# Softmax weights left unscaled in the three attention stages and turned by products with a scaled identity instead of transposes

## The reference

```python
def sink_softmax(logits, sink):
    m = jnp.maximum(jnp.max(logits, -1, keepdims=True), sink)
    e = jnp.exp(logits - m)
    return e / (jnp.sum(e, -1, keepdims=True) + jnp.exp(sink - m))
...
    orr = (jnp.einsum('bnkgim,bmkd->bnikgd', p[..., :N_META], vm)
           + jnp.einsum('bnkgij,bnjkd->bnikgd', p[..., N_META:], vband))
...
        p = jax.nn.softmax(jnp.concatenate([l_sel, l_own], axis=-1), axis=-1)
        o = (jnp.einsum('hqnj,hqnjd->hqd', p_sel, v_g.astype(jnp.float32))
             + jnp.einsum('hqk,hkd->hqd', p_own, v_own.astype(jnp.float32)))
```

## Time and profile before

| | us |
|---|---|
| median of 3 runs | 1254.89 |
| lowest, highest run | 1254.25, 1257.13 |
| the profiled execution | 1257.42 |
| its span, first to last instruction | 1255.6 |
| PE busy in the span | 1227.6 |
| DVE busy | 872.0 |
| ACT busy | 671.9 |

### The profile page before, as it was taken

How to read it: one execution, slowest core, us unless ns; L and a number is a source line. 1 busy time by engine, 2 the same in 40 slices (tenths; PEclk the granted TensorE clock), 3 DMA queues, 4 the chain that set the end, 5 groups by cost and what they waited for, 6 DMA issues and landing times.

```text
span 1255.6 us, 27652 instructions
## 1 busy us (share of the span) xinstructions
PE 1227.6 (98%) x10492; PEld 1194.4 (95%) x10492; DVE 872.0 (69%) x1585; ACT 671.9 (54%) x1210; POOL 179.5 (14%) x214
## 2 busy tenths in 40 slices
PE   7999999999999989999999999999999999999997
PEld 7889999999999879999999999999999879999997
DVE  7687578777645869888656667866455797766443
ACT  7766445555433756555545555655444586655432
POOL 0343050000012224000011004100011105000100
PEclk9999999999999999999999999999999999999999
DMA  7323257765544236555644444655555523655552
GB/s 290 102 86 102 85 159 211 209 194 197 195 149 145 85 106 215 185 183 192 225 170 132 138 152 136 202 184 185 184 187 182 185 85 117 201 184 180 189 186 68
DMA packets 60455, 205.89 MB, mean 164 GB/s; under 512 B 6096, under 2 KB 14544, under 8 KB 60240
## 3 DMA queue, kind: packets, MB, share of 16 engines
q1 hardware_dynamic: 56048, 200.33, 49.1%
q10 hardware_dynamic: 4320, 4.35, 1.1%
HBM read 200.46 MB, written 4.19 MB: 163 GB/s over the span
## 4 chain that ended last, share of the span: by engine, by line
PE 87%; DVE 7%; ACT 3%; issue 1%; DMA 1%; POOL 0%; ACTq 0%; DVEq 0%; SPq 0%
PE bank L317 27%; PE bank L319 26%; PE bank L318 26%; DVE w_lo L271 1%; DVE cb L684 1%; PE bank L1623 1%; PE bank L1613 1%; PE bank L1600 1%; DMA raw<-w_mix_in 1%; ACT w_hi L262 1%; ACT sm_s L1680 1%; DVE sm_d L1638 0%; PE bank L1269 0%; ACT sm_d L1680 0%; PE bank L1275 0%
## 5 line engine op out<-in xcount | busy, mean ns | idle before, releaser
L271 DVE TENSOR_TENSOR w_lo<-raw,w_hi 128x1024 fp32r<-128x1024 f32 (+1 forms) x357 | 458.1, 1284 | 195.1 <-ACT w_hi L262 194.5
L262 ACT ACTIVATE w_hi<-raw 128x1024 fp32r<-128x1024 f32 (+1 forms) x357 | 386.4, 1085 | 286.7 <-PE bank L319 278.5
L317 PE MATMUL bank<-x_hi,w_hi 128*128 128x256 f32 (+2 forms) x1776 | 511.4, 288 | 8.1 <-DVE x_lo L393 7.8
L319 PE MATMUL bank<-x_hi,w_lo 128*128 128x256 f32 (+2 forms) x1776 | 505.2, 284 | 0.0
L318 PE MATMUL bank<-x_lo,w_hi 128*128 128x256 f32 (+2 forms) x1776 | 505.1, 284 | 0.0
L317 PEld LDWEIGHTS bank<-x_hi,w_hi 128*128 128x128 f32 x1776 | 336.2, 189 | 10.5 <-DVE w_lo L271 7.7
L319 PEld LDWEIGHTS bank<-x_hi,w_lo 128*128 128x128 f32 x1776 | 336.1, 189 | 0.0
L318 PEld LDWEIGHTS bank<-x_lo,w_hi 128*128 128x128 f32 x1776 | 335.2, 189 | 0.5
L317 PE MATMUL bank<-m_hi,w_hi 128*128 128x256 f32 x512 | 144.1, 281 | 0.0
L318 PE MATMUL bank<-m_lo,w_hi 128*128 128x256 f32 x512 | 144.1, 281 | 0.0
L319 PE MATMUL bank<-m_hi,w_lo 128*128 128x256 f32 x512 | 144.1, 281 | 0.0
(11 more groups left out here) (331 smaller groups left out, 1686.9 us busy)
## 6 DMA issues: line engine op xcount, KB each, us to landing
raw<-w_up SPq DMA_DIRECT2D x88, 512.0 KB, 3.4
raw<-w_mlp_up SPq DMA_DIRECT2D x64, 512.0 KB, 4.2
raw<-w_mlp_down SPq DMA_DIRECT2D x64, 512.0 KB, 3.4
raw<-w_down SPq DMA_DIRECT2D x32, 704.0 KB, 4.0
raw<-w_mix_in SPq DMA_DIRECT2D x29, 512.0 KB, 3.4
raw<-w_moba_in SPq DMA_DIRECT2D x24, 512.0 KB, 3.7
raw<-w_swa_in SPq DMA_DIRECT2D x12, 512.0 KB, 3.3
raw<-w_mix_out SPq DMA_DIRECT2D x8, 512.0 KB, 3.2
```

The costliest lines, as they stand in the source:

```text
L262: nc.scalar.activation(w_hi[:, slot, 0:WIDTHS[g]], raw[:, slot, 0:WIDTHS[g]], ACT.Copy).then_inc(hi_ready, 1)
L271: nc.vector.tensor_tensor(w_lo[:, slot, 0:WIDTHS[g]], raw[:, slot, 0:WIDTHS[g]], w_hi[:, slot, 0:WIDTHS[g]].bitcast(F32), ALU.subtract).th ...
L317: nc.tensor.matmul(out, whi, xh, start=(chunk == 0), stop=False)
L319: mm = nc.tensor.matmul(out, wlo, xh, start=False, stop=end)
```

## The change

The exponentials stay as ACT wrote them. DVE builds, for each head and query group, a diagonal matrix: the identity times the reciprocal of each row's sum, into a new buffer `dg` (two pairs deep, laid over `gb` and `cb`). `pair_turn` then multiplies each 128x128 block with its diagonal matrix, which turns and scales it in one product, where it was a transpose with the identity.

```diff
+        dg = sb_alias("dg", [P, 2, 2, 2, P], gb)
...
-                for dst, c in ((0, at.c0 + at.first), (P, at.first), (2 * P, at.first + P)):
-                    tr = nc.tensor.transpose(TURN_BANKS[j][:, dst:dst + P], at.slot(u)[:, c:c + P], ident)
+                for dst, c, x in ((0, at.c0 + at.first, 1), (P, at.first, 0), (2 * P, at.first + P, 0)):
+                    tr = nc.tensor.matmul(TURN_BANKS[j][:, dst:dst + P], at.slot(u)[:, c:c + P],
+                                          dg[:, p % 2, j, x, :], start=True, stop=True)
...
+        def pair_diagonal(dve, at, p, j, n):
+            u = 2 * p + j
+            if p > 1:
+                at.wait(dve, "turned", 2 * p - 2)
+            at.wait(dve, "rec", u + n)
+            nc.vector.tensor_tensor(dg[:, p % 2, j:j + n, :, :],
+                                    ident.unsqueeze(1).unsqueeze(1).to_broadcast([P, n, 2, P]),
+                                    at.st[:, u:u + n, 6:8].unsqueeze(3).to_broadcast([P, n, 2, P]),
+                                    ALU.mult).then_inc(at.s["p"], 2 * n)
+
         def pair_norm(dve, at, p):
...
+            at.wait(dve, "exp", 4 * p + 4)
+            nc.vector.reciprocal(at.st[:, 2 * p:2 * p + 2, 6:8],
+                                 at.st[:, 2 * p:2 * p + 2, 4:6]).then_inc(at.s["rec"], 2)
+            pair_diagonal(dve, at, p, 0, 2)
...
-                swa.wait(dve, "rec", u + n)
+                pair_diagonal(dve, swa, p, j, n)
...
-                    st_s[:, u:u + n, 6:8].unsqueeze(3).to_broadcast([P, n, 2, META]), ALU.mult)
...
+                    st_s[:, u:u + n, 6:8].unsqueeze(3).to_broadcast([P, n, 2, META]), ALU.mult
+                    ).then_inc(S("smx_ready"), n)
...
+                pe.wait_ge(S("smx_ready"), 2 * p + 2)
```

More of the change, by code:

```diff
@@ L1646, in pair_reduce @@
                                             ALU.max, ALU.mult).then_inc(at.s["negmax"], 1)
-        def pair_norm(dve, at, p):
[L1649 to L1662, removed]
+        def pair_diagonal(dve, at, p, j, n):
[7 more added lines that the diff above has]
+                                    ALU.mult).then_inc(at.s["p"], 2 * n)
+        def pair_norm(dve, at, p):
+            at.wait(dve, "exp", 4 * p + 4)
+            nc.vector.reciprocal(at.st[:, 2 * p:2 * p + 2, 6:8],
+                                 at.st[:, 2 * p:2 * p + 2, 4:6]).then_inc(at.s["rec"], 2)
+            pair_diagonal(dve, at, p, 0, 2)
         def pair_low(dve, at, p):
```

## The result

The changed kernel takes 1269.83 us (median of 6 runs, 1268.22 to 1272.99) where the kernel before takes 1254.77 beside it (6 runs, 1254.25 to 1259.68). The ratio on record is 1.0107, with an interval from 1.0091 to 1.0123: slower by 1.1%. The two medians alone would give 1.0120. The profiled execution of the changed kernel took 1269.51 us, with a span of 1267.5; that of before took 1257.42, so between the two profiles 12.1 us were lost.

What follows compares the result with a forecast made beforehand. PE, busy for 98% of the span, was taken as the bound nearly everywhere; 5.5 (block attention) + 3.7 (last stage) + 2.4 (sliding window) = 11.6 us on 1254.89 gave 1266.5 us, range 1261 to 1271.

Steps and rivals of the forecast that it cites:

- the signs that were to show the prediction wrong: Six turn instructions a pair, PE waiting in block attention, or a wait for `p` or `smx_ready` before the turns.
- The price of the product: PE's turns: a block costs 0.223 us instead of 0.109, so 0.69 more a pair and 16.5 in all if unhidden.
- The operation on DVE: DVE's scaling: one two-tensor operation over 512 columns, taken at 0.69 us, replaces four multiplications of 1.01 us a pair.
- the rival built on it: DVE: at 0.85 us the new operation, with the joint waits, costs up to 3 us more, 1269.5 us; chance 0.09.
- DVE's gain of 0.32 a pair: DVE's scaling in each pair gets 0.32 us shorter, 0.16 at the other end of the bounds.
- Block attention: Middle of the three stages: PE never waits, so eight turns at 0.69 us more cost 5.5 us.
- The rival that the weights pace this stage: Block attention is paced by its weights, not PE, so its 5.5 us are hidden: 1261.0 us; chance 0.05.
- Last stage: Eight turns cost 5.5 us, less what waits for DVE absorb, plus 0.1 for a later first turn: 3.7 us.
- the slack of 0.6: Last stage: waiting for DVE absorbs 0.6 us of PE's 0.69 longer turn, at each of two turns.
- Sliding window: PE's longer turns, partly absorbed by waits, cost 3.8 us; a vanished clock drop returns 1.4: 2.4 us.
- Turn 3: Sliding-window stage: the wait of 0.41 us absorbs part of the 0.69, so it pays 0.3 us.
- The low clock behind turn 6: Sliding-window stage: the drop goes because the wait before it shrinks to 0.8 us, gaining 1.4; rival that it stays: 0.18.

Runs made afterwards that it cites:

- plain products: The kernel before with its transposes written as products with the plain identity, nothing else changed: 1271.13 us, ratio 1.0104.
- products twice: The changed kernel with each of the 144 products issued twice into the same place: 1303.1 us, ratio 1.0367.
- the diagonal with transposes: The changed kernel with PE transposing by the plain identity again; DVE still builds the diagonal, unused, so weights stay unscaled: 1255.54 us, ratio 0.9992.
- the rounded version: The changed kernel with exponentials (in tiles of their own) and diagonal in the rounded type fp32r: 1256.29 us, ratio 1.0002.

## Why the prediction was right, step by step

The mechanism held: PE's second instruction for each product is the loss. Of the signs that were to show the prediction wrong one did come, at two of 24 turns: a wait for the diagonal (`p`), 0.16 us before the first turn of the sliding window and 0.59 before the first of the last stage.

**The price of the product** was the step that everything hung on, and it held: 96 instructions a stage, 0.223 us for a product, 1.50 to 1.61 us for twelve in a row. The Trainium skill, in the table of terms of "TensorE: Matmul & The Clock Gate", gives the transpose mode as four times faster for float32. The trace does not agree: 0.223 to 0.109 us is a factor of two, and both doublings (plain products, products twice) bear it out.

**The operation on DVE** took 0.692 us, the end of its bounds that was chosen; the 0.85 and the rival built on it fall. The Trainium skill, in "VectorE: DVE Perf Modes", the section on the TRN2 errata, has a formula for a float32 two-tensor add that gives 691 ns at 512 columns. The trace agrees, though both operands are spread out here and the operation is a multiplication.

**DVE's gain of 0.32 a pair** was too large where it counts: the round that DVE sets became 0.22 shorter (the diagonal with transposes). The trace shows where the rest went: in the last stage DVE's next operation starts 0.92 us behind the reciprocal where it started 1.13 behind it, because the new operation follows the reciprocal by 0.31 us where the first multiplication followed it by 0.21. In the end it did not matter, since PE's longer round took its place.

**Block attention**: 5.2 in place of 5.5. PE never waits, as said, but a turn lengthened the pair's interval by 0.65 us and not by 0.69. The turn itself grew as forecast: from its start to the first product of the tile behind it was 699.65 - 699.08 = 0.57 us and is 704.77 - 703.52 = 1.25, so 0.68 more. The other 0.03 came off the pair's remaining rows; why is not shown. The rival that the weights pace this stage falls with 85.00 of 85 us busy.

**Last stage**: 2.9 in place of 3.7. The mechanism was right (waits for DVE take up part of PE's longer round), and so was the slack of 0.6 ahead of the two turns with rounds of 3.71 us: PE's product ahead of the turn at 1028.15 started at 1027.48, 0.67 us before it, where 0.06 is enough in the changed kernel (1034.27 to 1034.33). Mis-sized was the turn's own growth of 0.69. In the kernel before, PE's next row behind the turn at 1028.15 is this:

```profile
1029.09 0.87 PE L1623 MATMUL bank<-pt_d,vrow_d 128*64 128x256 f32 x8
```

That is 0.94 us behind the turn's start; in the changed kernel it is 1035.81 - 1034.33 = 1.48, only 0.54 more. With the diagonal and transposes, where both heads are released at once, the same stretch is 1022.32 - 1021.52 = 0.80, and the turn's row lasts 0.87 us where it lasted 1.01. So the turn of before held some 0.14 us of waiting inside it, for the scaling of the second head. With 0.54 - 0.6 = -0.06 the two rounds became 3.65, as measured. The rounds to 1024.44 and 1037.00 of the earlier trace rows paid 0.34 and 0.25, near to what was said, three others paid 0.54 to 0.59 in place of 0.69, and the last turn its 0.71. The 0.1 for the later first turn did not come: the wait there is longer (0.59, before 0.37), but the stretch ahead of it grew by 0.63, and by the same 0.63 with the plain products, where the wait is 0.37.

**Sliding window**: 3.8 in place of 2.4, the largest miss, and the one step that failed by its mechanism. Term by term, with the turns' intervals before and after:

- *Turn 3* was to pay 0.3, by counting its wait of 0.41 as slack. It paid 0.72 (6.94 to 7.66), and the wait stayed at 0.41. The wait hangs on PE itself: DVE's small step stands behind `pair_low`, which waits for ACT's `y_hi`, which waits for PE's values of pair 2, and those stand behind the longer turn of pair 2. The kernel with every product twice bears this out: its wait before turn 3 is again 0.41, and its interval 440.62 - 431.62 = 9.00 us, the whole 1.34 of its longer turn more. The prediction had seen such a loop for turn 7, and not here. Taking `pair_low` out of it brought 0.2 us back and showed the next link, GpSimd's `lrq`.
- *Turn 4* paid 0.48 where 0.45 was said. *Turn 6* paid 0.48 over the two intervals from turn 4 where 0.3 was said; its wait came down to 0.92, forecast 0.8.
- *Turn 0* came 0.18 us later, with a wait of 0.16 for the diagonal. The wait stands in every kernel with the diagonal and in neither of the two without. Whether the 0.18 is that wait is not shown: turn 0 begins anywhere between 413.34 and 416.28 us in the seven traces.
- *The low clock behind turn 6* went, as forecast, but was worth less. With transposes and no low clock, the interval from turn 6 to turn 7 is 5.38 us where it was 6.24, so 0.86 came back and not 1.4; the wait before turn 7 had taken 0.41 of it (0.81 to 1.22). With the plain products that wait stayed at 0.79, and there the drop was worth near to what was said: the interval is 465.14 - 459.39 = 5.75 us although the turn is 0.7 longer, so 6.24 + 0.7 - 5.75 = 1.2 came back. What the prediction left out is that this wait grows: it is 1.10 to 1.25 us in every kernel with the diagonal. By which link it grows is not shown. And the reason given for the drop's going, the shorter wait before turn 6, is not shown. With the diagonal and transposes PE stood still for 1.66 us at the same place and the clock did not fall; in the rounded version it stood still for 1.62, and the clock fell only behind the wait of turn 7. Why it falls where it falls stays open.

**The total**: 12.1 us between the profiles, where the sum was 11.6; the misses of the stages (+1.4, -0.3, -0.8) nearly cancel, so that the sum came out this close is partly luck. The changed kernel's median is 3.3 us above the forecast, and the two medians beside each other differ by 15.1. By the ratio the loss is 13.4 us, with an interval from 11.4 to 15.4, which holds both the 11.6 and the 12.1; the kernel before itself had medians of 1254.77, 1257.34 and 1257.4 in the three comparisons. How much of the 3.3 is such scatter, and how much a loss that the two profiles don't show, the runs don't tell.

## What to carry to other kernels

Before an operation is folded into a matmul, count the instructions that the matmul becomes in the trace: here a float32 product of 128x128 is two and a transpose is one, and on an engine that was busy for 98% of the span most of their price was paid (12.1 of 16.5 us here), while what was taken off an engine with a third of its time free was not paid back. And look inside the work before: part of a turn's time can be a wait that the change removes. A wait on the bound engine is slack for its own longer work only if the chain behind the wait does not begin at that engine; follow it back to its start before it is counted. Where the shorter mantissa of the rounded type can be afforded, the folding cost nothing that could be measured here.

## What the hardware did that was not expected

Where the granted clock falls differs between runs of like kernels. Before, it was at the lower level (1.2 GHz) behind turn 6 of the sliding window. In the plain-products kernel and in the one with diagonal and transposes it was not, with waits of 1.12 and 1.66 us there. In the rounded version it was at the lower level for at least the 12 us from 1020 on, behind a wait of 0.59 us at 1019.33. The changed kernel has a wait of the same 0.59 before the same turn and the full clock behind it; the kernel with every product twice has it too, and the lower clock behind it. Three of the rounded version's rounds took 3.88, 5.39 and 4.98 us there; the kernel with transposes has 2.17, 2.99 and 3.49, so it cost some 5.6 us, more than the 2.1 us that the forecast gave DVE's relief at the most.
